# Gated linear attention of layer 2: near blocks placed by mask, its first part inside the value projection, the output projection begun in its tail, waits reordered

## The reference, cut to what matters

```
g = log_sigmoid(z @ w_gate + b) / 16        # per token and key channel, <= 0
S_t = diag(exp(g_t)) S_{t-1} + k_t v_t^T ;  o_t = S_t^T q_t     # context state carried to the latents
o = o_forward + o_backward
y = (rms_norm(o per head) * silu(og)) @ w_o
```

## Time and profile before

| | |
|---|---|
| median of 3 runs | 2618.81 us (2612.16 to 2623.81) |
| the profiled execution, its own time | 2617.47 us |
| its span, first to last instruction | 2615.7 us |
| mean granted TensorE clock | 0.976 |
| value projection ends on PE | 1586.1 us from the span's start |
| last score part | 1703.98 us |
| output projection starts | 1716.0 us |

### The profile page before, as it was taken

One profiled execution on the slowest core, in us unless ns is written; L12 is line 12 of the kernel. 1 busy time (PEld: TensorE's weight loads), 2 busy tenths in 40 slices (PEclk: granted clock), 3 DMA queues, 4 the chain that ended last, 5 costly groups with the idle time before them and its releaser, 6 DMA issues. The chain is left out here.

```text
span 2615.7 us, 38016 instructions
## 1 busy us (share of the span) xinstructions
PE 2447.6 (94%) x15310; PEld 1966.2 (75%) x15310; DVE 1399.0 (53%) x2162; ACT 1134.9 (43%) x1936; POOL 333.4 (13%) x270
## 2 busy tenths in 40 slices
PE   6989899999999889999999997889999999978997
PEld 3655777778789558777788887777777788947997
DVE  2475565443443766555534335756545435476874
ACT  3365543333342565333323443445333324366663
POOL 0000311111100003111102002322111012002111
PEclk8999999999999999999999998999999999998998
DMA  7611356653232002656532320014656434603663
GB/s 243 212 38 59 112 169 182 185 179 103 78 99 86 25 23 66 186 178 185 175 97 83 104 81 26 2 49 126 187 178 185 136 99 88 160 21 93 183 184 98
DMA packets 500851, 311.32 MB, mean 119 GB/s; under 512 B 24178, under 2 KB 499618, under 8 KB 500548
## 3 DMA queue, kind: packets, MB, share of 16 engines
q1 hardware_dynamic: 498048, 307.39, 39.9%
q10 hardware_dynamic: 2628, 1.50, 0.2%
HBM read 307.80 MB, written 1.05 MB: 118 GB/s over the span
## 5 line engine op out<-in xcount | busy, mean ns | idle before, releaser
L1510 PE MATMUL bank<-h_hi,slab_hi 128*128 128x512 f32 (+1 forms) x2416 | 857.9, 355 | 37.9 <-DVE slab_lo L946 26.0
L1510 PE MATMUL bank<-h_lo,slab_hi 128*128 128x512 f32 (+1 forms) x2416 | 835.8, 346 | 0.0
L1510 PE MATMUL bank<-h_hi,slab_lo 128*128 128x512 f32 (+1 forms) x2416 | 835.3, 346 | 0.0
L946 DVE TENSOR_TENSOR slab_lo<-slab_raw,slab_hi 128x1024 fp32r<-128x1024 f32 (+1 forms) x388 | 538.8, 1390 | 542.6 <-ACT slab_hi L521 541.5
L521 ACT ACTIVATE slab_hi<-slab_raw 128x1024 fp32r<-128x1024 f32 (+1 forms) x388 | 401.5, 1036 | 524.1 <-PE bank L1510 271.2
L1510 PEld LDWEIGHTS bank<-h_hi,slab_hi 128*128 128x128 f32 x2416 | 464.0, 192 | 149.2 <-issue 89.6
L1510 PEld LDWEIGHTS bank<-h_hi,slab_lo 128*128 128x128 f32 x2416 | 464.4, 192 | 55.7
L1510 PEld LDWEIGHTS bank<-h_lo,slab_hi 128*128 128x128 f32 x2416 | 464.5, 192 | 50.0 <-issue 0.5
L915 ACT ACTIVATE conv<-bank,prm 128x512 f32<-128x512 f32 (+1 forms) x176 | 127.3, 723 | 362.7 <-PE bank L1510 362.4
L1510 PE MATMUL bank<-g_hi,slab_hi 128*128 128x512 f32 (+1 forms) x770 | 269.3, 350 | 2.1 <-ACT res_t L572 2.1
L1510 PE MATMUL bank<-g_hi,slab_lo 128*128 128x512 f32 (+1 forms) x770 | 267.2, 347 | 0.0
(11 more groups left out here) (210 smaller groups left out, 2770.1 us busy)
## 6 DMA issues: line engine op xcount, KB each, us to landing
slab_raw<-in_mod_w SPq DMA_DIRECT2D x192, 512.0 KB, 4.6
slab_raw<-in_ffn_w_up SPq DMA_DIRECT2D x176, 512.0 KB, 4.5
slab_raw<-in_ffn_w_down SPq DMA_DIRECT2D x64, 512.0 KB, 4.1
slab_raw<-in_ffn_w_down SPq DMA_DIRECT2D x32, 384.0 KB, 3.6
slab_raw<-in_b_w_qkv SPq DMA_DIRECT2D x24, 512.0 KB, 3.7
slab_raw<-in_c_w_in SPq DMA_DIRECT2D x24, 512.0 KB, 3.7
slab_raw<-in_d_w_qkv SPq DMA_DIRECT2D x24, 512.0 KB, 6.7
slab_raw<-in_a_w_qkv SPq DMA_DIRECT2D x12, 512.0 KB, 5.3
```

What stands on the lines that cost most here:

```text
L946: nc.vector.tensor_tensor(wlo[slot][:, 0:w], raw[of][:, 0:w], whi[slot][:, 0:w].bitcast(f32), ALU.subtract).then_inc(s_lo, 1)
L1510: ins = mm(out, l, r, start=first and n == 0, stop=last and n == 2)
```

## The change

1. `exponents(0)` and `exponents(1)` run inside the value projection, in front of its pieces 14 and 15, into banks 4 to 7, with `decays(0)`, `decays(1)` on ACT, `query(0)` on DVE and part 0 of k on POOL. The gates of unit 0 are rounded there into buffers of their own (`g_first`), and the `decay` buffers no longer lie over the context's gates; `k_part` and `q_part` 1 and 2 do, so part 1 of both waits for the fourth rest.
2. On DVE the latent gates' rests stand behind `query(1)` and `query(2)`.
3. `place_near` is four full-width products and sums a unit: `near`, repeated four times, times a 0/1 block mask into `spread`, then added to `scores`. The far bank's diagonal is cleared once. `scores` has one buffer a block, so ACT copies the far scores in part 3 (before: part 1), after the unit before was used.
4. `q_dec` has two buffers.
5. The steps of a finished head are spread wider: second square and second gating in part 0 of the next half, sum of squares and root in part 2 (before: 0 and 1), norm in part 3 (before: 2), rounding and rest in parts 0 and 1 of the next unit (before: both in part 3). `update` stands ahead of `output`.
6. Behind the last score PE runs k = 0 to 3 of output tiles 0, 1 and 2 (`out_begin`), one ahead of the last `output`, one ahead of the last sum of squares (now in bank 7), one behind it; k = 4 to 7 follow in their place.

```diff
@@ places
+        spread = [place(f"spread{p}", [P, P // TILE, TILE], at=spread_at) for p in range(2)]
+        g_first = [place("g_first_hi", [P, T], f32r, at=mod_row_at), place("g_first_lo", [P, T], f32r, at=list(prm_at))]
-        q_dec = place("q_dec", [P, 2, 2 * CH], at=gla_at)
+        q_dec = [place(f"q_dec{s}", [P, 2, 2 * CH], at=gla_at if s == 0 else prm_at) for s in range(2)]
@@ ACT, value projection, then loop
+                        act.wait_ge(S["gate"], 4)
+                        round_gates(0)
...
+                    if g == 3:
+                        for r in range(PARTS_AHEAD):
+                            decays(r)
...
-                    if q == 1:
+                    if q == 3:
                         far_scores(u)
                     if half == 0 and hd and q == 3:
-                        head_squares(hd - 1)
-                    if half == 1 and hd and q == 1:
+                        head_square(hd - 1, 0)
+                    if half == 1 and hd and q == 0:
+                        head_square(hd - 1, 1)
+                    if half == 1 and hd and q == 2:
                         head_root(hd - 1)
-                    if half == 1 and hd and q == 3:
-                        head_hi(hd - 1)
+                    if half == 0 and hd >= 2 and q == 0:
+                        head_hi(hd - 2)
@@ DVE
-                    for b in range(0, P, TILE):
-                        ins = nc.vector.tensor_copy(scores[u % 2][p][b:b + TILE, b:b + TILE], near[p][b:b + TILE, :])
+                        nc.vector.tensor_tensor(spread[p][:], near[p][:].unsqueeze(1).broadcast_to([P, P // TILE, TILE]),
+                                                diagonal[:], ALU.mult).then_inc(S["spread"], 1)
...
+                        nc.vector.tensor_tensor(scores[p][:].rearrange("p (b i) -> p b i", i=TILE),
+                                                scores[p][:].rearrange("p (b i) -> p b i", i=TILE), spread[p][:], ALU.add
+                                                ).then_inc(S["scores"], 1)
...
+                nc.vector.memset(bank[3][:, 0:2 * CH], 0.0).then_inc(S["far_cleared"], 1)
-                    if r < 2:
-                        gates_rest(4 + 2 * r)
-                        gates_rest(5 + 2 * r)
-                    query(r)
+                    if r:
+                        query(r)
+                    if r in (1, 2):
+                        gates_rest(2 + 2 * r)
+                        gates_rest(3 + 2 * r)
@@ PE
+                    14: lambda: exponents(0), 15: lambda: exponents(1)})
...
+                pe.wait_ge(S["far_copied"], 2 * C_UNITS)
+                pe.wait_ge(S["rs_ready"], C_HEADS - 1)
+                out_begin(0)
                 output(C_UNITS - 1, 0)
                 output(C_UNITS - 1, 1)
+                out_begin(1)
                 squares_sum(C_HEADS - 1)
+                out_begin(2)
```

More of the change, by code:

```diff
@@ L420, in build_program @@
         n_parts = C_PARTS * C_UNITS
-        exponent_uses = [("part", r, d) for r in range(PARTS_AHEAD) for d in (BWD, FWD)]
+        exponent_uses = []
         for r in range(n_parts):
@@ L756, in end_decay, with decays, round_gates @@
                                      ).then_inc(S["end_exped"], 1)
+            def decays(r):
+                S = att[2]
+                for d in (BWD, FWD):
+                    act.wait_ge(S["sums"], 2 * r + d + 1)
+                    if d == BWD and r >= PART_BUFS:
+                        act.wait_ge(S["q_prod"], r - PART_BUFS + 1)
+                        act.wait_ge(S["k_prod"], r - PART_BUFS + 1)
+                        if (r - PART_BUFS) % C_PARTS == C_PARTS - 1:
+                            act.wait_ge(S["q_dec"], (r - PART_BUFS) // C_PARTS + 1)
+                    nc.scalar.activation(
+                        decay[r % PART_BUFS][:, d, :, :].rearrange("x l (p t) -> x p l t", p=2),
+                        exponent_bank("part", r, d)[:].rearrange("x (p l t) -> x p l t", p=2, l=2),
+                        ACT.Exp, scale=1 / C_NORMALIZER).then_inc(S["decay"], 1)
+            def round_gates(k):
+                S = att[2]
+                u = split_order[k]
+                dst = h_hi[:, u, :] if k else g_first[0][:]
+                nc.scalar.activation(by_gate(dst), unit_gates(u), ACT.Copy).then_inc(S["g_hi"], 1)
             def gla_tables():
@@ L1321, in head_lo @@
                                                 h_hi[:, 2 * hd + v, :].bitcast(f32), ALU.subtract).then_inc(S["o_lo"], 1)
-                for k in range(4):
+                dve.wait_ge(s_free["dve"], freed[start["wo", 2][1] - 1][1])
+                nc.vector.memset(bank[3][:, 0:2 * CH], 0.0).then_inc(S["far_cleared"], 1)
+                for k in range(1, 4):
                     gates_rest(k)
@@ L1337, in gla @@
                         reduce_near(u - 1)
+                    if q == 0 and half == 1 and hd:
+                        head_gated(hd - 1, 0)
                     if q == 1 and u:
-                        place_near(u - 1, 0)
-                        place_near(u - 1, 1)
+                        place_near(u - 1)
+                    if q == 1 and half == 0 and hd >= 2:
+                        head_lo(hd - 2)
                     if q == 2 and half == 0:
@@ L1770, in end_sums, with exponents @@
                    ).then_inc(S["end_full"], 1)
+            def exponents(r):
+                S = att[2]
+                u, q = divmod(r, C_PARTS)
+                if q == 0:
+                    pe.wait_ge(S["g_hi"], split_order.index(u) + 1)
+                    pe.wait_ge(S["g_lo"], split_order.index(u) + 1)
+                for d in (BWD, FWD):
+                    out = exponent_bank("part", r, d)
+                    before = exponent_before("part", r, d) if r >= PARTS_AHEAD else None
+                    if r < PARTS_AHEAD:
+                        pe.wait_ge(S["k_end"], 5 + r)
+                        pe.wait_ge(S["end_exped"], 5 + r)
+                    if before:
+                        pe.wait_ge(S[before[0]], before[1])
+                    for p in range(2):
+                        g = slice(CH * (2 * p + d), CH * (2 * p + d) + CH)
+                        for n, x in enumerate((h_hi[:, u, :], h_lo[:, u, :]) if u else (g_first[0], g_first[1])):
+                            ins = mm(out[:, 2 * CH * p:2 * CH * p + 2 * CH], x[:, g],
+                                     summed[:, d, 2 * q:2 * q + 2, :].rearrange("p l t -> p (l t)"), start=n == 0, stop=n == 1)
+                    ins.then_inc(S["sums"], 1)
             def qkv_gla(n, fg):
@@ L1793, in qkv_gla, with out_tiles, out_begin @@
                     9: lambda: end_sums(1, BWD), 10: lambda: turn_keys(2), 11: lambda: end_sums(2, FWD),
[L1794 removed]
+                    12: lambda: turn_keys(3), 13: lambda: end_sums(3, BWD),
+                    14: lambda: exponents(0), 15: lambda: exponents(1)})
+            def out_tiles(e, k0, k1, done=None):
+                n, out = at_slab["wo", 2][e], bank[(start["wo", 2][1] + e) % 4]
+                split_ready(n)
+                for k in range(k0, k1):
+                    pe.wait_ge(att[2]["o_lo"], k + 1)
+                    wc = slice(k * P, (k + 1) * P)
+                    ins = three(out[:], whi[n % SLOTS][:, wc], wlo[n % SLOTS][:, wc], h_hi[:, k, :], h_lo[:, k, :],
+                                k == 0, k == DT - 1)
+                if done:
+                    ins.then_inc(done, 1)
+            def out_begin(e):
+                group_free(start["wo", 2][1] + e)
+                out_tiles(e, 0, 4)
             def gla():
                 S = att[2]
[L1797 to L1812 removed]
                 def score(r):
@@ L1873, in gla @@
                 pe.wait_ge(s_free["dve"], freed[start["wo", 2][1] - 1][1])
-                pe.wait_ge(S["summed"], 2)
-                for r in range(PARTS_AHEAD):
-                    exponents(r)
+                pe.wait_ge(S["far_cleared"], 1)
                 for r in range(n_parts):
```

224 lines of the change are left out of this document (106 added, 118 removed).

## The result

| | before | after |
|---|---|---|
| median of 7 runs each | 2618.04 us | 2599.05 us (2593.40 to 2603.72) |
| the profiled execution: time, span | 2617.47, 2615.7 | 2597.88, 2596.1 |
| attention stage, slab split 204 to slab split 222 on ACT | 251.48 | 228.12 |
| value projection ends on PE | 1586.1 | 1589.4 |
| last score part | 1703.98 | 1687.40 |

The ratio after to before is 0.9926 (95%: 0.9915 to 0.9937): 19.4 us less, 16.5 to 22.3. Forecast were 2590 us and 28.7 less; the time lies inside the range of 2578 to 2605. (The prediction's 2579 to 2606 are the same bounds, counted from the median and not from the profiled execution.)

A forecast was written before the change was run, and what follows sets the result against it. Bound: PE standing still, in the middle through the handing over between PE and DVE. Start 11.0, middle 12.4 and tail 5.3 sum to 28.7 us off 2617.47, 2588.8; median 1.3 higher, 2590 us; 8-in-10 range 2578 to 2605.

The forecast's parts named there:

- start: Start of attention: update behind part 3 at 1600.1 against 1611.13, 11.0 us won (8 to 12).
- first stretch: Middle, from 1611.13 to 1634.73, ahead of the full heads: 23.6 us comes out at 21.1, 2.5 us won.
- two full heads: Middle: periods of 28.69 and 29.90 us fall to 24.5 (23.4 to 27), winning 4.2 and 5.4 us.
- last four parts: End of the middle: the sum of squares moves closer to their end, 0.3 us won.
- tail: Behind the last score: begun output tiles fill PE's gaps and speed the last outputs, 5.3 us won (3.5 to 6.3).
- Hiding `q_dec`: Middle: with two buffers, DVE makes it while waiting for nothing; `q_dec`, both gatings and query cost PE 0.9 us before.
- forecast signs: Last score about 1681, heads 24 to 25 us, no DVE wait at `q_dec`, PE's query wait under 5 us, not 16.7.
- price of DVE's work in the middle: Middle: eight full-width operations at 0.22 us, 1.8 in all, replace 16 copies of 3.4; DVE drops 1.6 us a head.
- my layout: One head's order laid out by hand: 28.0 us before, 23.4 after (22.0 of PE work plus 1.4), stretched to 24.5.
- first rival: DVE becomes the bound: POOL and DVE exclude each other, period 27.5, middle wins 1.2 + 2.4 + 1, 2598 us; chance 0.2.
- third rival: PE's gaps under 1 us keep its clock at 2.4 GHz, period 22.5, 2583 us; chance 0.12.
- PE gets full: Gaps under 1 us, clock at 2.4 GHz: period 22.5, middle wins 17.6, start 12, tail 6.3, 2583 us; chance 0.12.

The follow-up runs named there:

- u_start: Changed kernel with exponents, decays and query of the start behind the value projection and the latent gates' rests ahead of queries 0 and 1 again: 2609.87 us.
- u_tail: Changed kernel without the three begun output tiles, all eight tiles running whole behind the last sum of squares: 2606.93 us, ratio 0.9961 to the kernel before.
- u_head: Changed kernel with a finished head's squares, gatings, sum, root, norm, rounding and rest back at their old places: 2606.03 us, ratio 0.9947 to the kernel before.
- u_place: Changed kernel with eight 32x32 copies a unit again in place of the mask products and sums: 2600.75 us, ratio 0.9925 to the kernel before.
- x_pool: Changed kernel with about half of POOL's k products left out, output not the reference's: 2591.91 us, ratio 0.9903 to the kernel before.

## Why the prediction was right in kind and its gain 9 us too high

| step | forecast us | measured us | where read |
|---|---|---|---|
| start | 11.0 | 10.0 | 97.37 to 87.38 |
| first stretch | 2.5 | 0.7 | 23.34 to 22.68 |
| two full heads | 4.2, 5.4 | 3.1, 4.4 | table above |
| last four parts | 0.3 | -0.1 | 11.00 to 11.11, last update to last score |
| tail | 5.3 | 5.3 | last score to slab split 222, 61.19 to 55.88; 24 products of 0.227, begun 0.1 later |
| stage | 28.7 | 23.4 | |
| whole | 28.7 | 19.4 (16.5 to 22.3) | ratio |

**Right.** Start: the two `exponents` cost the value projection 0.95 us each with no stop ahead of pieces 14 and 15; PE stood 2.73 us before the first product (2.5 forecast) and ran at half clock soon behind it, as forecast. `u_start` confirms the size at 8.6. It fell 1.0 us short on PE, not on DVE: from its first product at 1592.22 to the update at 1602.54 PE has no stop, and its own work, at half clock from 1593.16 to 1599.99, takes 10.3 us where my times (1590.6 to 1600.1) left it 9.5. DVE was dearer than I had it (1.90 us for query 2 beside POOL, 0.8 forecast; 2.36 for the two rests before it, 2.2 forecast), but that shows only behind the update: PE waits 0.77 us for a query at 1607.45 and 0.76 for the scores at 1608.67. The tail is right, and `u_tail` gives it back with 6.0. Hiding `q_dec` and spreading the head's steps were named as the cause of the middle, and the spreading it was (`u_head`); the forecast signs of it, DVE's wait at `q_dec` gone and PE's wait for queries down from 16.7, came in, the latter at 6.9 and not under 5. The last score came at 1687.40, entry 1.5 us late included, and not at 1681.

**The step that failed is the price of DVE's work in the middle.** I took 0.22 us for each full-width product and so let DVE drop 1.6 us a head. Measured are 0.278 for the product and 0.582 for the sum, 3.2 us for the eight, against 3.4 for the copies: it drops 0.2. With all else kept, the placing is worth 0.1 and 0.35 us a head (`u_place`). The larger part is the free-running price that I used for the queries that PE waits for: 0.8 for the pair behind the norm, measured 1.82, so a stop of 1.14 where my layout had 0.2. And I left out PE's wait for the finished score block, 0.75: I had the first block usable after 0.65, the chain of waits has 0.26 and 0.89 for it. Together my layout had stops of 1.4 us a head, the trace has 3.19. `x_pool` shows the cause: with about half of POOL's products away the stops fall to 1.29, near what the layout had, and the period to 23.86, near its 23.4. The price could have been read before the change. The kernel before has the same pair beside POOL, ahead of its longest stop:

```profile
1650.67 1.82 DVE L1258 TENSOR_TENSOR q_part<-qk,decay 128x256 f32<-128x256 f32 x2
```

The eight copies that the prediction took as the trace's sign of such holding up read one operand each; this pair reads two, like the products that were to be priced.

So the first rival was part of the truth. Its mechanism, POOL and DVE shutting each other out, is shown, but it acts on the queries and on one sum in two, not on all eight products: a head came out 1 us above the forecast, not 3. That its 2598 us is nearly the measured time is chance; the measured time is the sum of a start 1 us below the rival's, a middle better than the rival's (8.1 us won, not 4.6), and a loss elsewhere that it did not contain.

**The layout was not confirmed by the old heads, and the heads' gain is in part luck.** I took 28.0 against 28.7 and 29.9 as a check and stretched 23.4 to 24.5 by the 3 to 7% that was missing. But the 28.0 held 22.0 of work and 6.0 of stops, where the trace has 4.75 of stops and, by the windows, 1.6 and 2.8 us of clock. So the layout had the stops 1.2 us too long before and 1.8 too short after: it let them shrink by 4.6 us, and they shrank by 1.6. That the heads still won 3.1 and 4.4 of 4.2 and 5.4 us comes half or more from the clock, which the sum left out and only the third rival had. In the changed kernel the clock is 1.00, so none of the 2.1 us between 23.4 and 25.5 is clock; `x_pool` takes 1.7 of them away. The rival *PE gets full* had the clock right (1.00 in every window behind the start) and the stops wrong: they stayed under 1.2 us, not under 1, and the period is 25.5, not 22.5.

The first stretch won 0.7 and not 2.5 us: it had a clock of 1.00 before, no norm and no sum of squares, so nothing of what helped the full heads was there to be removed. PE's stops of 0.4 us or more in it went from 2.73 to 2.15 us. One `q_dec`, the old placing or the old head's steps leave the stretch at 22.69, 22.71 and 22.75 us, so none of the three brought the 0.7; the order of `update` and `output` was not undone alone, and which part did it is not shown.

**Between stage and whole** lie 4 us. 3.8 of them are in the two profiled executions as well: ACT reaches split 204 1.5 us later, and slabs 292 to 311, of the query, key and value projection of layer 3 that waits for its weights, take 75.16 instead of 73.55; the rest is spread. In all 14 traces, with the same code at these places, entry lies between 1513.7 and 1520.8 us and that projection takes 73.6 to 78.5. The kernel before has the two earliest entries, and 73.55 and 74.79 for the projection. Whether that is chance, or the changed kernels lose a microsecond or two there for a reason, stays open; the interval of the ratio (up to 22.3 us) reaches the 22.3 to 23.4 of the stage.

**What stays open** is when the clock falls in the middle. It is not the length of the stops alone: with the same four stops the changed kernel kept 1.00 in two traces and `u_start` fell three times. It costs 1.5 to 3 us a head, as much as any edit tried, and no run here separates what decides it. So the stage of `u_start` gives the start's value plus 4 us of clock, and a kernel's ranking by one edit carries such a step in it.

## What to carry to other kernels

Where two engines hand work to each other, order the queue so that the operand the other one waits for goes first, and spread long chains of a finished step (norm, rounding, rest) over several parts: that, and not cheaper instructions, was the middle's gain, half of it or more by way of the clock. Price a DVE operation on such a path by its row beside POOL's work, not by its free-running row, check a hand layout against stops and clock separately and not against the period alone, and try an edit alone before believing that its busy time is its worth. To see a few microseconds, compare a stage between two marks that lie outside the stretches fed by transfers, with the granted clock beside it.

## What the runs showed of the hardware

- Two DVE queries of 128x256 take 0.74 us in a row alone and 1.82 beside POOL's products (each ended 0.28 us after the product that it met); the norm of two 128x512 takes 1.29 or 2.10; one 128x128 sum from SBUF about 0.29 or 0.89.
- A 128x128 product that repeats its input four times by a step of zero costs 0.278 us, a sum of the same size that repeats nothing 0.28 to 0.29 alone: the repeated reading has no price of its own that shows. The clearing of 128x256 in PSUM took 0.27.
- The granted clock fell to half in stretches with stops of 0.6 to 1.15 us in one kernel (`u_start`), and did not fall in another with the same stops; in the middle the same stretches came back when a kernel was traced again.
- The places fed by transfers differ by up to 7.1 us (entry of the stage) and 4.9 us (layer 3's projection) between executions of the same code.
